# Reordering one head's work on VectorE, moving a small copy to ScalarE, and reordering the first expert of an mLSTM and mixture-of-experts layer

## The reference, cut to what matters

```
z = x @ w_in                      # q, k, v, o, gates, pooling input, gate_A, gate_B
A = mLSTM(q, k, v, i, f)          # 4 heads of 256; h = num / max(|den|, exp(-m)); LayerNorm per head
C_new = decay * C_old + (w * k)^T v   # 256x256 state per head: one for the prompt, one for each sample sequence
x = LN(ALPHA * x + mix(A, B) @ w_out)
for each of 16 experts, on the rows routed to it (top 2 of one group):
    h = silu(x @ w_gate) * (x @ w_up);  y = h @ w_down
x = LN(ALPHA * x + sum of gate * y)
```

## Time and profile before

| what | value |
|---|---|
| median of 3 runs | 1023.2 us (1022.01 to 1023.42) |
| the profiled execution, its own time | 1021.46 us |
| its span | 1020.3 us |
| TensorE busy | 889.7 us (87%), mean granted clock 0.933 |
| VectorE busy | 606.3 us (59%) |
| ScalarE busy | 385.1 us (38%) |
| GpSimd busy | 101.5 us (10%) |
| chain that ended last | PE 80%, DVE 13%, issue 3%, DMA 2%, ACT 2% |
| bytes moved | 195.26 MB, mean 191 GB/s, 412 to 421 GB/s in the expert loop |

### The profile page before, as it was taken

One profiled execution on the slowest core, in us unless ns is written; L12 is line 12 of the kernel. 1 busy time (PEld: TensorE's weight loads), 2 busy tenths in 40 slices (PEclk: granted clock), 3 DMA queues, 4 the chain that ended last, 5 costly groups with the idle time before them and its releaser, 6 DMA issues.

```text
span 1020.3 us, 14646 instructions
## 1 busy us (share of the span) xinstructions
PE 889.7 (87%) x5949; PEld 806.3 (79%) x5949; DVE 606.3 (59%) x841; ACT 385.1 (38%) x382; POOL 101.5 (10%) x86
## 2 busy tenths in 40 slices
PE   6999999899998987999998996289889999999700
PEld 6999889788897987999998996268778888888600
DVE  3643453735556362033234245579999999999557
ACT  3521122121331313222222005157667787777301
POOL 3000000000000000101101011201011111110065
PEclk9989999999999989999999997589999999999955
DMA  9651360543606142122223612559899999999152
GB/s 284 211 207 42 94 206 1 176 124 94 206 1 183 55 130 89 42 83 84 83 91 130 281 63 108 185 186 319 315 382 400 421 412 414 415 415 393 67 175 87
DMA packets 79535, 195.26 MB, mean 191 GB/s; under 512 B 3889, under 2 KB 56841, under 8 KB 67192
## 3 DMA queue, kind: packets, MB, share of 16 engines
q1 hardware_dynamic: 72312, 168.88, 45.9%
q0 software_dynamic: 7168, 25.58, 6.6%
HBM read 167.65 MB, written 26.79 MB: 191 GB/s over the span
## 4 chain that ended last, share of the span: by engine, by line
PE 80%; DVE 13%; issue 3%; DMA 2%; ACT 2%; POOL 0%; POOLq 0%; SPq 0%; DVEq 0%; ACTq 0%
PE psum L419 23%; PE psum L421 22%; PE psum L420 22%; DVE split_lo L1354 2%; PE psum L1777 2%; PE psum L1796 2%; PE psum L1787 1%; PE psum L1995 1%; PE psum L1825 1%; DVE x L1623 1%; DMA xg<-x_rows,idx_i 1%; ACT split_hi L904 1%; DVE last_lo L1354 1%; PE psum L1811 1%; DVE onehot L1459 1%
## 5 line engine op out<-in xcount | busy, mean ns | idle before, releaser
L419 PE MATMUL psum<-x_hi,split_lo 128*128 128x272 f32 x704 | 212.0, 301 | 1.4 <-ACT ht L780 1.4
L421 PE MATMUL psum<-x_hi,split_hi 128*128 128x272 f32 x704 | 204.9, 291 | 0.0
L420 PE MATMUL psum<-x_lo,split_hi 128*128 128x272 f32 x704 | 204.8, 291 | 0.0
L1354 DVE TENSOR_TENSOR split_lo<-raw,split_hi 128x2048 fp32r<-128x2048 f32 x72 | 163.3, 2286 | 16.6 <-ACT split_hi L904 15.0
L414 DVE TENSOR_TENSOR split_lo<-raw,split_hi 128x2048 fp32r<-128x2048 f32 x35 | 80.1, 2290 | 137.1 <-ACT split_hi L395 136.9
L904 ACT CAST split_hi<-raw 128x2048 fp32r<-128x2048 f32 x72 | 137.5, 1913 | 54.3 <-PE psum L421 54.3
L419 PEld LDWEIGHTS psum<-x_hi,split_lo 128*128 128x128 f32 x704 | 135.6, 193 | 4.9 <-issue 2.7
L420 PEld LDWEIGHTS psum<-x_lo,split_hi 128*128 128x128 f32 x704 | 135.6, 193 | 1.5 <-issue 1.0
L421 PEld LDWEIGHTS psum<-x_hi,split_hi 128*128 128x128 f32 x704 | 135.3, 192 | 0.0
L395 ACT CAST split_hi<-raw 128x2048 fp32r<-128x2048 f32 x35 | 66.7, 1905 | 60.1 <-PE psum L421 58.4
L419 PE MATMUL psum<-split_hi,xgl 128*128 128x512 f32 x192 | 79.4, 414 | 2.8 <-DVE xgl L1515 2.8
(11 more groups left out here) (358 smaller groups left out, 1795.8 us busy)
## 6 DMA issues: line engine op xcount, KB each, us to landing
raw<-in_w_e_gate_dram SPq DMA_DIRECT2D x32, 1024.0 KB, 8.1
raw<-in_w_e_up_dram SPq DMA_DIRECT2D x32, 1024.0 KB, 7.9
raw<-in_w_e_down_dram SPq DMA_DIRECT2D x32, 1024.0 KB, 7.5
raw<-in_w_in_dram SPq DMA_DIRECT2D x26, 1024.0 KB, 7.0
cb<-in_state_C_dram SPq DMA_DIRECT2D x8, 1024.0 KB, 8.1
out_dram<-cb SPq DMA_DIRECT2D x8, 1024.0 KB, 5.9
y_slots<-ys POOLq DMA_DIRECT2D x16, 512.0 KB, 8.1
y_slots<-x_hi POOLq DMA_DIRECT2D x2, 2048.0 KB, 11.3
```

Of the source, the lines that this page charges most:

```text
L419: nc.tensor.matmul(out, a_lo, b_hi, start=first, stop=False)
L420: nc.tensor.matmul(out, a_hi, b_lo, start=False, stop=False)
L421: return nc.tensor.matmul(out, a_hi, b_hi, start=False, stop=last)
L1354: v.tensor_tensor(lo, raw2[:, n % MOE_SLOTS, :], hi.bitcast(F32), ALU.subtract).then_inc(w_lo, 1)
```

## The change: what it does, and the diff

In a head, VectorE's low part of chunk 3h + 7 (C_U + 1 in the last head) moves from ahead of the fifth normalisation to behind the second group of sample states; the copy of the prompt's values (unit V) moves from behind the last group to ahead of it. The four copies of the sample values (unit W) move from VectorE to ScalarE, ahead of its high part of chunk 3h + 8 (ahead of the units B for head 0). In the first expert, TensorE's `rows_in(1)` moves from behind the four `up` to behind the second; ScalarE's `split_x(1)` and VectorE's `x_low(1)` move ahead of chunk 5; VectorE's `times_up` moves ahead of chunks 6 and 7. SyncE waits for the first gather to have landed before it issues the load of chunk 6 and all behind it.

```
@@ SyncE, ahead of the expert loads
         sp.dma_start(lnb[:], ln2_b[0].partition_broadcast(P)).then_inc(ln_in, 16)
+        sp.wait_ge(g_in[0], 16)
         with sp.Fori(1, NE - 1) as e:
@@ ScalarE
+        def sample_values(h):
+            j = Z["W", h]
+            ac.wait_ge(z_done, j + 1)
+            for g in range(4):
+                last = nc.scalar.copy(ve[g * NS:(g + 1) * NS, PT, 0:DH], wide(j)[0:NS, 0, 0:DH])
+            last.then_inc(z_free[j % 2], 1)
...
         dense_split_hi(ac, 4)
+        sample_values(0)
         for h in range(H):
             j = Z["B", h]
...
             dense_split_hi(ac, 3 * h + 7)
+            sample_values(h + 1)
             dense_split_hi(ac, 3 * h + 8)
...
         gate_sigmoid()
+        ac.wait_ge(xt_done, 2)
+        split_x(1)
         expert_hi(5, w_used, 2)
         expert_hi(6, w_used, 3)
         expert_hi(7, w_used, 4)
-        ac.wait_ge(xt_done, 2)
-        split_x(1)
@@ VectorE
-            j = Z["W", h]
-            ve_.wait_ge(z_done, j + 1)
-            for g in range(4):
-                last = v.tensor_copy(ve[g * NS:(g + 1) * NS, PT, 0:DH], wide(j)[0:NS, 0, 0:DH])
-            last.then_inc(z_free[j % 2], 1)
...
                 gate_low(3)
-                dense_split_lo(ve_, C_U + 1)
-            else:
-                dense_split_lo(ve_, 3 * h + 7)
             normalised(h, 4)
             variance(h)
             states(h, 2, 6)
             norm(h)
-            states(h, 6, H_PER_HEAD)
+            states(h, 6, 10)
+            dense_split_lo(ve_, C_U + 1 if last_head else 3 * h + 7)
+            states(h, 10, 14)
+            if not last_head:
+                values(h + 1)
+            states(h, 14, H_PER_HEAD)
             states_end(h)
...
             else:
-                values(h + 1)
                 dense_split_lo(ve_, 3 * h + 8)
...
         silu(0)
+        ve_.wait_ge(xgh_ok, 2)
+        x_low(1)
         moe_split_lo(5, C_MOE + 6)
+        ve_.wait_ge(w_used, 4)
+        times_up()
         moe_split_lo(6, C_MOE + 7)
         moe_split_lo(7, C_MOE + 8)
-        ve_.wait_ge(w_used, 4)
-        times_up()
-        ve_.wait_ge(xgh_ok, 2)
-        x_low(1)
@@ TensorE
             up(0, n, 2 + n // 2, n % 2)
-        pe.wait_ge(g_in[1], 16)
-        rows_in(1)
+            if n == 1:
+                pe.wait_ge(g_in[1], 16)
+                rows_in(1)
```

## The result

The changed kernel takes 998.55 us (median of 4 runs, 998.29 to 999.60), the kernel before beside it 1022.82 (4 runs, 1022.01 to 1023.42): a ratio of 0.9771, 95% interval 0.9752 to 0.9791. The forecast was 1007.1, with a range from 1003.5 to 1013.6. The profiled execution took 998.32 (span 997.1), at a mean granted clock of 0.943 where it was 0.933.

The account below looks back on a forecast made before the run. TensorE, with 80% of the chain of waits, was taken to bound the kernel. Gains of 4.9 + 4.7 + 0 + 0.5 + 2.6 + 3.4 = 16.1 us took 1023.2 to 1007.1, range 1003.5 to 1013.6.

Parts of the forecast that it names:

- The waits in the heads: Ahead of the sample states: TensorE's waits go, 1.64 us in each of heads 0 to 2 and 3.2 in the last.
- The border: Between heads, three times: S1 starts 1.3 us earlier, a new 1.1 us stall behind ScalarE's queue cancels it; gain 0.
- The prediction's estimate from the Trainium skill: At the borders: four W copies on ScalarE cost 1.43 us, making the sum about 0.6 us worse over three borders.
- The units B: Ahead of head 0: W copies on ScalarE end earlier, in time for the first B copy; gain 0.5 us.
- The first gather: Ahead of the first expert: with later loads held back, the gather lands 2.6 us earlier.
- The prediction's estimate with the Trainium skill's fixed cost of 2 us: At the first gather: fixed cost plus transfer lands it at 651.4, making the sum 0.8 us better.
- The first expert: VectorE's chain decides: chunk 9's low part starts 25.9 us behind the first product, not 29.3; gain 3.4 us.
- the clock in the last head +1.5: Behind the last head's first sample-state group: with no idle time TensorE's clock stays up, gaining 1.5 us.
- (a): First expert: late loads make ScalarE wait, the expert gain is given back, only the heads' 10.1 remain: 1013.1 us; chance 0.08.
- (d): Loop: loads take over and turns lengthen, making the kernel slower than before, about 1026 us at 19.1 a turn; chance 0.03.
- (b): Borders and gather: S1's 1.3 us carries through at each border and the gather lands at 650.7: 1001.6 us; chance 0.07.
- (c): Heads: the moved low part makes the third state group late, shrinking the heads' 9.6 to 3.2: 1013.5 us; chance 0.05.

Follow-up runs that it names:

- e6: Changed kernel with the four sample-value (W) copies back on VectorE, behind the last group of states: 997.70 us, ratio 0.9763.
- e7: Changed kernel with ScalarE's high part of chunk 3h + 8 behind the next head's decays, VectorE's low part behind its first scores: 998.09 us, ratio 0.9757.
- e12: Changed kernel with W's copies back on VectorE and chunk 3h + 8 split only behind the next head's decays: 998.56 us, ratio 0.9781.
- e8: Kernel before plus only SyncE's wait for the first gather: 1019.64 us, ratio 0.9977.
- e1: Changed kernel's heads alone, with SyncE and the first expert as in the kernel before: 1006.88 us, ratio 0.9854.
- e3: Kernel before with only VectorE's low part moved behind the second group of sample states in every head: 1010.43 us, ratio 0.9886.
- e4: Changed kernel without SyncE's wait for the first gather: 1000.50 us, ratio 0.9807.
- e9: Kernel before measured again, unchanged, as a control: 1022.06 us, ratio 0.9997.
- e5: Changed kernel measured again, unchanged: 1003.58 us, ratio 0.9808.
- e10: Changed kernel with VectorE's low part back ahead of the fifth normalisation in heads 0 to 2: 1011.82 us, ratio 0.9893.
- e11: Changed kernel with VectorE's low part back ahead of the fifth normalisation in the last head alone: 1006.96 us, ratio 0.9863.
- e2: Changed first expert and SyncE's wait alone, with the heads as in the kernel before: 1015.16 us, ratio 0.9932.

## Why the prediction was right and where it was wrong

**The waits in the heads: right.** Forecast 1.64 a head for three and 3.2 in the last; measured 1.71 three times and 3.27. The 1.5 of clock behind the last head's first group came as 1.54. The low part fits behind the second group, as worked out.

**The border: right in kind, a little off in size.** The wait at S1 (1.02 us) and the new one at L419 for `ht` (1.05, forecast 1.1) are there, and the stall did change its name. The four copies took 1.48 us and not 1.28, so a border loses 0.16 instead of 0. The prediction's estimate from the Trainium skill ("VectorE: DVE Perf Modes", section on the TRN2 errata) had the four at 1.43 and three borders at a loss of about 0.6 us. It was nearer than my reading of two copies of 258 columns: the trace has 1.48, and 0.16 a border is 0.5 for three. e6, e7 and e12 show that the queue is the cause.

**The units B** gave 0.23 instead of 0.5.

**The first gather: right in kind, too small.** Forecast 2.6, measured 3.2 to 3.6 in all nine profiles with the wait; it lands 6.4 us after issue (6.1 in e8), not 7. The prediction's estimate with the Trainium skill's fixed cost of 2 us ("DMA: Bandwidth & Descriptors", section on the GpSimd path) put it at 6.2 and the end 0.8 earlier; the traces agree with that sum. About 1 us of it comes and goes without the wait (e1, e3 and e4 gain 1.2, e9 0.4), so the wait itself is worth 2 to 3 us.

**The first expert: right.** Forecast 3.4 through VectorE's chain, measured 3.65, with `hs` awaited 0.78 us (forecast 0.9) and chunk 9's low part at S + 25.8 (forecast 25.9). e4, e5, e6, e10 and e11 have 3.4 to 3.8; e2, e7 and e12 only 2.3 to 2.4. That too goes with the clock: it is at the lower level in the routing ahead of the first expert, and in e2, e7 and e12 it stays there until S + 6 instead of S + 3 or 4. Windows of 7.08 us from S, in the changed kernel and in e7:

```profile
641.64:648.72 7.08, 7.08 (x25) 5.69 (x26) 0.55 (x1) 1.92 (x1) 0.00 (x0) 0.78 1.00 377
643.53:650.61 7.08, 7.08 (x18) 5.56 (x19) 0.00 (x0) 1.50 (x1) 0.00 (x0) 0.56 1.01 393
```

The window has 0.56 to 0.58 in these three and 0.74 to 0.80 in the other six, and `hs` comes at S + 15.6 to 15.8 instead of S + 14.2 to 14.6.

**What failed: the sum has TensorE's clock in one place only.** It takes "the clock in the last head +1.5" and prices every other wait at its length in us. Each of the four profiles with the old heads has two or three stretches at the lower clock there, of 1.4 us or more each: one behind the 3.2 us wait, the rest behind waits of 1.64 us or at borders. None was left in eight profiles without the waits ahead of the sample states, and three came back when e10 and e11 put those waits back. Against the mean of the four old profiles (-1.4 in the last column) the change is worth 10.95 + 1.4 = 12.4 in the heads, where 9.6 were forecast. Waits and borders make 5.1 + 3.3 - 0.5 = 7.9 of it, so the clock makes 4.5, of which 1.5 stood in the sum. The same omission stands at the entry into the loop: in the kernel before, 2.2 us of waiting for `hs` at 742.27 are followed by the stretch at 744. It is worth 1.6 us, gained in 7 of 9 profiles with the new first expert, and in those without at most 0.3 (e1, e3, e8, e9). I had written of TensorE's lead in the first expert that the rest of it becomes waiting, and looked at no clock beyond.

**What was luck.** 12.4 in the heads, 3.3 at the gather (the changed kernel's two profiles), 3.2 in the first expert (the mean of nine), 1.2 at the entry (1.6, 7 times in 9) and 0.3 ahead of the heads make 20.4, an estimate from the ledger. The ten runs of the changed kernel have a mean of 1001.3, 51 runs of the kernel before on the chips of the experiments 1022.0: 20.7. So some 4.5 us of the miss are steps that I got wrong (3.0 of clock in the heads, 1.2 at the entry, the gather up, the borders down), and the other 3.6 of the 24.3 are what the first measurement had above these means. In the two profiled executions of the changed kernel such a difference lies almost wholly in where the clock fell outside the heads (6.8 us, see e5); that it was so in the other runs is not shown, as they have no trace. The range's lower end, 1003.5, would have been missed by the mean as well. It took in an error of each term, but no term for the clock and none for executions that differ by several us.

**The rivals.** (a) and (d): no high part of an expert waited for a DMA, and turns stayed at 17.76. (b): the border paid nothing and the gather came at 6.4 us; its 1001.6 is near the mean for another reason. (c): no group of states came late.

**Open.** What makes the clock fall behind one wait of 1.64 us and not behind the next is not settled, nor why a border has such a stretch only in heads that also have that wait, nor why in seven of the fourteen profiles it stayed low for 10 us at the start of head 0 (about 69 to 80 us) and cost some 3 us there. That the first gather is faster by 1 us behind the new heads, with nothing changed at it, was not followed up. A kernel with the heads of e6 and a better start was not tried.

## What to carry to other kernels

When a wait of the engine that sets the time goes away, price the granted clock behind it too: read it in windows behind every wait, in more than one profiled execution, and give a wait its length plus the share of cases in which the clock fell times what that cost (here 1.64 + 6/15 x 1.5 = 2.2 us, an estimate from 15 cases). Before work moves to an idle engine, read what its queue must deliver next: here 1.5 us of copies on ScalarE, which was busy 38% of the time, used up a whole gain, and putting them back beat the change. And a difference of a few us between two profiles is the change's only when the same kernel, profiled twice, agrees with itself at that place.

## What was not expected of the hardware

Waits of 1.64 us, in which TensorE did nothing, were followed by a stretch at the lower clock in 6 of 15 cases, and in kernels without waits ahead of the sample states the clock stayed at 1.00 from 80 to 340 us in 8 of 8 profiles. So a kernel with fewer waits doesn't only wait less: between the same two times it also ran at the higher clock throughout, where the four profiles with the old heads have 7 to 14 us at the lower one.

The mean granted clock of a whole run shows this only roughly. Of 51 runs of the kernel before every one lies between 0.928 and 0.938, of ten runs of the changed kernel between 0.937 and 0.945, and in e11 0.934 goes with 1010.06 us and 0.944 with 1003.22. But two runs of the changed kernel at the same 0.943 took 998.32 and 1004.97 us. The mean counts stretches in which TensorE waits anyway like those on its path, so it takes windows to tell what a stretch cost.

The four copies of 32 x 256 from PSUM took 1.48 us on ScalarE and 1.70 us on VectorE, and yet the heads were 3.2 us shorter with them on VectorE (e6): here the faster engine for a piece of work was the wrong one to give it to.
